# Norm rows made in the projection, output weights split around the last store, and a modulation folded into the router's weights

## The reference

```python
h_lat = modulate(rms_norm(x, norm_g[l, 0]), mod_lat[0], mod_lat[1])
m_ctx, m_lat = hybrid_mixer(h_ctx, h_lat, w_in[l], ...)
x = x + mod_lat[2] * rms_norm(m_lat, norm_g[l, 1])

h_lat = modulate(rms_norm(x, norm_g[l, 2]), mod_lat[3], mod_lat[4])
y_lat = ec_moe(h_lat, router_w[l], exp_w_gate[l], exp_w_up[l], exp_w_down[l])
x = x + mod_lat[5] * rms_norm(y_lat, norm_g[l, 3])
```

## Time and profile before

| | us |
|---|---|
| runs | 1444.17, 1443.9, 1441.17; median 1443.9 |
| profiled execution | 1444.64 (span of the core's instructions 1442.9) |
| PE busy | 1291.1 (89%) |
| DVE busy | 780.1 (54%) |
| ACT busy | 468.2 (32%) |
| POOL busy | 230.2 (16%) |
| DMA, mean over the span | 188 GB/s |
| mean granted clock of TensorE | 0.955 of full |

### The profile page before, as it was taken

How to read it: one execution, slowest core, us unless ns; L and a number is a source line. 1 busy time by engine, 2 the same in 40 slices (tenths; PEclk the granted TensorE clock), 3 DMA queues, 4 the chain that set the end, 5 groups by cost and what they waited for, 6 DMA issues and landing times.

```text
span 1442.9 us, 13834 instructions
## 1 busy us (share of the span) xinstructions
PE 1291.1 (89%) x5008; PEld 748.6 (52%) x5008; DVE 780.1 (54%) x1102; ACT 468.2 (32%) x1101; POOL 230.2 (16%) x206
## 2 busy tenths in 40 slices
PE   6999999899999999899999878997079999999993
PEld 2444554445545555689889744454034444444441
DVE  4169888797874877487767555553910010010015
ACT  4335543542211112667766523333011101101122
POOL 0004111121000000174455200000010110101111
PEclk9999999999999999999999989997579999999996
DMA  9515354345223443366556644432749999999967
GB/s 367 124 29 177 114 153 138 95 141 153 88 87 103 84 88 79 81 185 189 180 171 186 240 161 174 157 134 100 266 165 350 327 341 342 324 341 338 330 228 173
DMA packets 207529, 270.64 MB, mean 188 GB/s; under 512 B 75053, under 2 KB 124198, under 8 KB 207462
## 3 DMA queue, kind: packets, MB, share of 16 engines
q1 hardware_dynamic: 187118, 210.97, 45.1%
q0 software_dynamic: 14272, 52.43, 12.1%
q10 hardware_dynamic: 6072, 6.35, 1.2%
HBM read 217.75 MB, written 51.97 MB: 187 GB/s over the span
## 4 chain that ended last, share of the span: by engine, by line
PE 59%; DMA 13%; DVE 12%; ACT 11%; issue 4%; SPq 2%; POOL 0%; POOLq 0%; ACTq 0%; DVEq 0%
PE ps L1820 25%; PE ps L1078 13%; PE ps L1097 6%; DMA arena<-g_dram 5%; DMA arena<-zt_dram 2%; DVE arena L2167 2%; PE ps L387 2%; ACT arena L524 2%; PE ps L1041 2%; DMA y_dram<-arena 2%; DMA arena<-ada_w 2%; ACT arena L533 2%; PE ps L1695 1%; PE ps L1773 1%; ACT arena L513 1%
## 5 line engine op out<-in xcount | busy, mean ns | idle before, releaser
L1820 PE MATMUL ps<-arena 128*128 128x512 f32 (+1 forms) x1072 | 424.8, 553 | 0.0
L1820 PEld LDWEIGHTS ps<-arena 128*128 128x128 f32 x1072 | 202.4, 191 | 202.4 <-issue 197.4
L1078 PE MATMUL ps<-arena 128*128 128x512 f32 x512 | 227.3, 597 | 1.4 <-ACT arena L1200 1.4
L2167 DVE SCALAR_TENSOR_TENSOR arena<-arena,taps 128x1024 f32<-128x1024 f32 x160 | 215.9, 1349 | 5.5
L1078 PEld LDWEIGHTS ps<-arena 128*128 128x128 f32 x512 | 96.7, 192 | 117.1 <-issue 115.1
L387 PE MATMUL ps<-arena 128*128 128x128 f32 x1080 | 135.5, 281 | 17.1 <-DVE arena L604 13.3
L387 PEld LDWEIGHTS ps<-arena 128*128 128x128 f32 x1080 | 130.4, 195 | 23.7 <-DVE arena L604 16.4
L1363 DVE TENSOR_TENSOR arena<-arena,ps 128x512 f32<-128x512 f32 x16 | 11.0, 688 | 224.4 <-PE ps L1078 224.4
L1041 PE MATMUL ps<-arena 128*128 128x512 f32 x256 | 115.6, 606 | 4.6 <-ACT arena L1149 4.6
L1097 PE MATMUL ps<-arena 128*128 128x512 f32 x256 | 113.3, 595 | 0.0
L1041 PEld LDWEIGHTS ps<-arena 128*128 128x128 f32 x256 | 48.3, 193 | 62.5 <-issue 55.8
(11 more groups left out here) (298 smaller groups left out, 1634.8 us busy)
## 6 DMA issues: line engine op xcount, KB each, us to landing
arena<-exp_w_gate SPq DMA_DIRECT2D x16, 2048.0 KB, 11.1
arena<-exp_w_up SPq DMA_DIRECT2D x16, 2048.0 KB, 9.1
arena<-exp_w_down SPq DMA_DIRECT2D x16, 2048.0 KB, 11.1
arena<-ada_w POOLq DMA_DIRECT2D x16, 1024.0 KB, 6.4
arena<-w_in SPq DMA_DIRECT2D x28, 512.0 KB, 5.2
arena<-ada_w SPq DMA_DIRECT2D x4, 2048.0 KB, 18.0
arena<-x SPq DMA_DIRECT2D x16, 512.0 KB, 6.6
arena<-g_dram SPq DMA_DIRECT2D x16, 512.0 KB, 4.7
```

The source lines that it names most:

```text
L1078: last = mm(ps[gu_bank[s] + j][:], xsT[s][:, k, :], ew[s][j][:, k, :], start=(k == 0), stop=(k == KD - 1))
L1820: last = mm(ps[3 * (m % 2) + gi][:, 0:w], wring[(m + 1) % NW][:, k, :], hT[:, k, o:o + w], start=(k == 0), stop=(k == KD - 1))
L2167: ins = v.scalar_tensor_tensor(accg, cin_l[ci % 2][:, j // 3:j // 3 + GR, j % 3:j % 3 + GW], tp[:, j:j + 1], accg, ALU.mult, ALU.add)
```

## The change

- The columns `rcol` of the norms are made on DVE between the scan's preparation and the first `v` convolution. There, the router's weights are also multiplied by the second modulation's gain (`rwg`). A new job `rows` in block `M_V0 + 2` = 21 transposes the columns into 32 rows, which ACT copies and stores to `rows_dram`, and multiplies the shift by the router's weights into `shifted` (eight products of 16 columns).
- In the tail, SP loads `rowv` and `row5` from there, spread over the partitions. The 32 transposes and eight copies go.
- `scan_over` goes from PE's and ACT's tails, and on DVE it moves behind `front_r(2)`. Tile 0's `front` moves into DVE's last scan step, ahead of `y_diag`.
- `w_out` lies in two separate halves. The first is loaded after the last use of the first direction's buffers, ahead of the last two scan stores, the second after the last but one store has landed, ahead of the last store.
- `front_r(t+1)` stands behind `front(t+1)` and so ahead of `back_sum(t-1)`.
- `h2` is only scaled by the root, no longer by the gain, and without the shift: the router uses `rwg` and adds `shifted`; ACT's copy of an expert's turned tokens applies gain and shift per column block, in four operations instead of one.
- ACT's squares go to another scrap buffer (`sqf` in place of `sqj`), in the places that the cut diff leaves out too.

```diff
@@ -59,6 +59,7 @@
     tok_dram = dram("tok_dram", (DN_H + 1, NT * P, P))
+    rows_dram = dram("rows_dram", (4 * (D // P), P))
@@ -263,11 +264,19 @@
             jobs[m] += [("late", i, 0)]
+        jobs[M_V0 + 2] += [("rows", 0, 0)]
...
+        rcol = arena[:, 49152:49152 + 4 * KD].rearrange("p (r k) -> p r k", r=4)
+        rowst = arena[0:4 * KD, 49152 + 4 * KD:49152 + 4 * KD + P]
+        rwg = arena[:, 49152 + 160:49152 + 160 + KD * E_N].rearrange("p (k n) -> p k n", k=KD)
+        shifted = arena[:, 49152 + 160 + KD * E_N:49152 + 160 + (KD + 1) * E_N]
@@ -677,6 +686,9 @@
                 if lat(own):
+                    if s == 2 * NS - 1:
+                        dve_front(dve, link, 0)
@@ -861,10 +873,14 @@
         h2T = [take(D).rearrange("p (k n) -> p k n", k=KD) for _ in range(2)]
-        rowv = take(3 * D).rearrange("p (r n) -> p r n", r=3)
+        rowv = take(D)
+        sqf = take(D)
+        sq, rs, sm = ([take(8) for _ in range(2)] for _ in range(3))
...
         at[0] = W0
-        wo = take(KD * D).rearrange("p (k n) -> p k n", k=KD)
+        wo = [take(KD * 512).rearrange("p (k n) -> p k n", k=KD) for _ in range(2)]
...
@@ -943,14 +957,25 @@
                 sp_.dma_start(xr[s], x_t[o]).then_inc(sem(f"xr_in{s}"), 16)
+            def load_wo(h):
+                sp_.dma_start(wo[h], wo_k[:, :, h * 512:(h + 1) * 512]).then_inc(sem(f"wo_in{h}"), 16)
+            def load_row(dst, r):
+                sp_.dma_start(dst, rows_dram[r * KD:(r + 1) * KD].rearrange("k p -> (k p)").unsqueeze(0).to_broadcast([P, D]))\
+                    .then_inc(sem("rowv"), 16)
...
             load(1)
-            for step in steps[-2:]:
-                scan_store(sp_, step)
+            sp_.wait_ge(sem("s_op"), turn(0, NL))
+            load_wo(0)
+            scan_store(sp_, steps[-2])
+            sp_.wait_ge(sem("st_o0"), 16 * NL)
+            load_wo(1)
+            scan_store(sp_, steps[-1])
+            sp_.wait_ge(sem("rows_out"), 16)
+            load_row(rowv, 0)
             scan_over(sp_)
-            for h in range(2):
-                sp_.dma_start(wo[:, :, h * 512:(h + 1) * 512], wo_k[:, :, h * 512:(h + 1) * 512])\
-                    .then_inc(sem(f"wo_in{h}"), 16)
+            load_row(row5, 3)
@@ -989,19 +1014,6 @@
             mm, tr = nc.tensor.matmul, nc.tensor.transpose
-            scan_over(pe)
-            for r in range(4):
-                if r >= 2:
-                    pe.wait_ge(sem("rowv"), r - 1)
-                elif r == 0:
-                    pe.wait_ge(sem("rcol"), 1)
-                for k in range(KD):
-                    last = tr(ps[2 * (r % 2) + k // 4][:, (k % 4) * P:(k % 4 + 1) * P], rcol[:, r, k:k + 1].to_broadcast([P, P]),
-                              ident[:])
-                last.then_inc(sem("rowps"), 1)
-            pe.wait_ge(sem("rowv"), 4)
...
@@ -1038,7 +1050,7 @@
                     for k in range(KD):
-                        last = mm(ps[2 + 2 * s + h][:], mixT[s][:, k, :], wo[:, k, h * 512:(h + 1) * 512],
+                        last = mm(ps[2 + 2 * s + h][:], mixT[s][:, k, :], wo[h][:, k, :],
@@ -1122,7 +1134,6 @@
             a = nc.scalar.activation
-            scan_over(act)
@@ -1131,9 +1142,9 @@
                 for h in range(DN_H):
-                    a(sqj[:, h * P:(h + 1) * P], fb[s][:, h * P:(h + 1) * P], ACT.Square, accum_out=sq[s][:, h:h + 1])
+                    a(sqf[:, h * P:(h + 1) * P], fb[s][:, h * P:(h + 1) * P], ACT.Square, accum_out=sq[s][:, h:h + 1])
                 for g in range(SSM_G):
-                    last = a(sqj[:, QK + g * 256:QK + (g + 1) * 256], fb[s][:, QK + g * 256:QK + (g + 1) * 256],
+                    last = a(sqf[:, QK + g * 256:QK + (g + 1) * 256], fb[s][:, QK + g * 256:QK + (g + 1) * 256],
...
@@ -1197,7 +1208,9 @@
                     act.wait_ge(sem("gu"), 2 * e - 2)
-                a(xsT[e % 2][:, 4 * h:4 * h + 4, :], heads(ps[0][:]), ACT.Copy).then_inc(sem("xsT"), 1)
+                for k in range(4 * h, 4 * h + 4):
+                    last = a(xsT[e % 2][:, k, :], ps[0][:, cols(k % 4)], ACT.Identity, scale=rcol[:, 1, k:k + 1], bias=rcol[:, 2, k:k + 1])
+                last.then_inc(sem("xsT"), 1)
@@ -1231,27 +1244,17 @@
+        def dve_front(dve, link, t):
+            v = nc.vector
+            s = t % 2
+            dve.wait_ge(sem(f"m_in{s}"), 64 * (t // 2 + 1))
+            link(v.tensor_tensor(fb[s], fb[s], bb[s], ALU.add))
+            link(v.tensor_tensor(heads(bb[s][:, QK:D], SSM_H), heads(xtok[:, ORD[t], :], SSM_H), bc(sbc[:, 48:56], SSM_P), ALU.mult))
+            link(v.tensor_tensor(fb[s][:, QK:D], fb[s][:, QK:D], bb[s][:, QK:D], ALU.add))
+            v.tensor_tensor(fb[s][:, QK:D], fb[s][:, QK:D], zb_[s], ALU.mult).then_inc(sem("merged"), 1)
...
             v = nc.vector
-            scan_over(dve)
-            m = mods[:, :, 0]
-            g = vcols[:, V_NG:V_CB].rearrange("p (r k) -> p r k", k=KD)
-            link(v.tensor_tensor(m[:, 2 * KD:6 * KD], m[:, 2 * KD:6 * KD], vcols[:, V_AB + 2 * KD:V_NG], ALU.add))
-            v.tensor_tensor(rcol[:, 0, :], m[:, 2 * KD:3 * KD], g[:, 1, :], ALU.mult)
-            v.scalar_tensor_tensor(rcol[:, 1, :], m[:, 4 * KD:5 * KD], 1.0, g[:, 2, :], ALU.add, ALU.mult)
-            v.tensor_copy(rcol[:, 2, :], m[:, 3 * KD:4 * KD])
-            v.tensor_tensor(rcol[:, 3, :], m[:, 5 * KD:6 * KD], g[:, 3, :], ALU.mult).then_inc(sem("rcol"), 1)
-            def front(t):
-                s = t % 2
-                dve.wait_ge(sem(f"m_in{s}"), 64 * (t // 2 + 1))
-                link(v.tensor_tensor(fb[s], fb[s], bb[s], ALU.add))
-                link(v.tensor_tensor(heads(bb[s][:, QK:D], SSM_H),
-                                     xtok[:, ORD[t], :].rearrange("p (h n) -> p h n", h=SSM_H),
-                                     bc(sbc[:, 48:56], SSM_P), ALU.mult))
-                link(v.tensor_tensor(fb[s][:, QK:D], fb[s][:, QK:D], bb[s][:, QK:D], ALU.add))
-                v.tensor_tensor(fb[s][:, QK:D], fb[s][:, QK:D], zb_[s], ALU.mult).then_inc(sem("merged"), 1)
@@ -1279,7 +1282,7 @@
                     hs_ = slice(h * 512, (h + 1) * 512)
-                    ins = v.scalar_tensor_tensor(x2[:, ORD[t], hs_], ps[2 + 2 * s + h][:], sm[s][:, 2:3], rowv[:, 0, hs_],
+                    ins = v.scalar_tensor_tensor(x2[:, ORD[t], hs_], ps[2 + 2 * s + h][:], sm[s][:, 2:3], rowv[:, hs_],
@@ -1292,21 +1295,20 @@
                     dve.wait_ge(sem("h2ps"), t - 1)
-                link(v.scalar_tensor_tensor(h2[s], x2[:, ORD[t], :], sm[s][:, 3:4], rowv[:, 1, :], ALU.mult, ALU.mult))
-                v.tensor_tensor(h2[s], h2[s], rowv[:, 2, :], ALU.add).then_inc(sem("h2"), 1)
-            front(0)
-            for r in range(4):
-                dve.wait_ge(sem("rowps"), r + 1)
-                dst = rowv[:, r, :] if r < 3 else row5
-                v.tensor_copy(dst[:, 0:512], ps[2 * (r % 2)][:])
-                v.tensor_copy(dst[:, 512:D], ps[2 * (r % 2) + 1][:]).then_inc(sem("rowv"), 1)
+                v.tensor_scalar(h2[s], x2[:, ORD[t], :], sm[s][:, 3:4], None, ALU.mult).then_inc(sem("h2"), 1)
+            front_r(0)
...
                 if t < NL:
-                    front_r(t)
...
                 if t + 1 < NL:
-                    front(t + 1)
+                    dve_front(dve, link, t + 1)
+                    front_r(t + 1)
+                if t == 1:
+                    scan_over(dve)
+                    dve.wait_ge(sem("rowv"), 16)
@@ -1314,7 +1316,7 @@
                     o = ORD[t - 2]
-                    v.tensor_copy(aff[:, o % 4 * 2 + o // 4, :], ps[1][:, 0:E_N]).then_inc(sem("lcopy"), 1)
+                    v.tensor_tensor(aff[:, o % 4 * 2 + o // 4, :], ps[1][:, 0:E_N], shifted, ALU.add).then_inc(sem("lcopy"), 1)
@@ -1800,6 +1802,12 @@
                                           start=True, stop=True)
+                    elif kind == "rows":
+                        pe.wait_ge(sem("rcol"), 1)
+                        tr(bank[0:4 * KD, 0:P], rcol.rearrange("p r k -> p (r k)"), ident[:])
+                        for k in range(KD):
+                            last = mm(bank[:, P:P + E_N], rcol[:, 2, k:k + 1].to_broadcast([P, P]), rw[:, k, :],
+                                      start=(k == 0), stop=(k == KD - 1))
@@ -1961,11 +1969,17 @@
                                  bank[:].rearrange("p (q g n) -> p q g n", q=2, g=SSM_G), ACT.Copy)
+                    elif kind == "rows":
+                        a(shifted, bank[:, P:P + E_N], ACT.Copy)
+                        last = a(rowst, bank[0:4 * KD, 0:P], ACT.Copy)
...
-                    if kind == "qk":
+                    if kind == "rows":
+                        act.wait_ge(sem("aux_used"), aux + 1)
+                        act.dma_start(rows_dram, rowst).then_inc(sem("rows_out"), 16)
+                    elif kind == "qk":
@@ -2241,6 +2255,15 @@
             dve.wait_ge(sem("g_dve"), 7)
+            mc = mods[:, :, 0]
```

(16 more changed lines are left out.)

## The result

| | before | after |
|---|---|---|
| median of runs, us | 1444.4 (20 runs) | 1453.2 (20 runs) |
| ratio | | 1.0054, 95% interval 1.0042 to 1.0066 |
| profiled execution, span, us | 1442.9 | 1448.0 |
| PE / DVE / ACT busy, us | 1291.1 / 780.1 / 468.2 | 1292.3 / 761.0 / 497.9 |

The changed kernel is slower by 0.5%, and the forecast was 1437.0. The profiled execution of after (1449.8) is one of its quicker ones, so its trace shows 5.1 us of a difference that is 8.8 us by the medians.

What follows compares the result with a forecast made beforehand. Bound: the tail's per-tile loop through load transfers, not PE. Handover 9.0, order -2.0, product 4.2, last h2 1.8, rows -2.0, copies -1.95, stores -2.0: 7.05 us gained, so 1437.0 us, range 1432.5 to 1441.5.

Steps and rivals of the forecast that it cites:

- rows in the projection: In the projection, PE's added transpose and eight 16-column products lie wholly on the path: 2.0 us lost, at most 3.
- handover, to A(2): Between scan and tail: tile 0 done 9.9 us sooner, 0.9 lost waiting for tile 2's loads: 9.0 us gained.
- A(2): In the tail's tile loop: the time at which DVE starts to merge tile 2; likewise for other tile numbers.
- new order on DVE, five loops: In the tail loop, scaling the next tile ahead of the sum adds 0.4 us per loop: 2.0 us lost.
- stores against loads, five loops: In the tail loop, earlier stores of h2 and x2 meet the next loads: 0.4 us per loop, 2.0 us lost.
- product of tile 7 behind A(7): In the tail, each product starts sooner after its tile's merge because h2 is ready earlier: 4.2 us gained, once.
- h2 of the last tile: At the stage's end, tile 7's h2 lies bare on the chain and gets shorter: 1.8 us gained.
- copies in the experts: In the experts, four ACT operations replace one, 0.65 us more per group, three groups bare: 1.95 us lost.
- rival 5: Tail loop: 1 MB of stores ahead of the loads' last bytes makes the kernel slower, 1448 at the bound; chance 0.04.
- c: Tail loop: extra time per loop from stores meeting loads; taken as 0.4 us, between 0 and 2.6.
- my bound of 2.6: Tail loop: most extra us per loop, if all 1 MB of stores goes ahead of the loads' last bytes, twice 1.3.
- Rival 3: Tail loop: stores and loads share alike, 1.85 us more overlap at half rate; 1439.4, up to 1441; chance 0.15.

Runs made afterwards that it cites:

- the second one: The changed kernel run again with no edit, beside the kernel before: 1454.97 us, ratio 1.0051.
- the run with the earlier loads: Changed kernel with the next tile's four loads issued ahead of the wait for the residual's buffer: 1434.24 us, ratio 0.991 to the kernel before.
- the kernel before with the hold: Kernel before, with GpSimd sending tile t's stores only after tile t+3's loads have landed: 1446.38 us, ratio 1.0009.

## Why the prediction was wrong

Step by step, in the profiled executions (plus is gained, us):

| step | forecast | measured |
|---|---|---|
| rows in the projection | -2.0 | -1.9 |
| handover, to A(2) | +9.0 | +8.0 |
| new order on DVE, five loops | -2.0 | -1.5 |
| stores against loads, five loops | -2.0 | -8.0 |
| product of tile 7 behind A(7) | +4.2 | +2.9 |
| h2 of the last tile | +1.8 | +1.8 |
| copies in the experts (-2.7), first gate product (-1.0) | -1.95 | -3.7 |
| head, projection and scan otherwise | 0 | -3.0 |
| sum | +7.05 | -5.4 (spans: -5.1) |

**The step that failed** is the paragraph "An unknown: stores against loads". That earlier stores lengthen the wait for the next loads was named, and so was rival 5, which decides from c = 1.8 and had 0.04. The term c was mis-sized: I took 0.4; in the profiled execution it was 1.6 (9.5 us less the order's 1.5, over five), in the second one 2.7 ((109.9 - 95.0) / 5 less 0.3), past my bound of 2.6; with the stores at once on ScalarE's queue it was 3.6. Two reasonings led there. I read the landings of 6.08 to 7.07, with stores 2.75 us behind, as a measure of how much overlap costs, though the stores hardly overlap the loads there: in the transfer view of before, 909 to 917.04, that is until 1.4 us behind the store's issue, 1.75 of the loads' 2.10 MB have gone, and no packet of the stores. In after it is 1.09 MB at the same distance from the store's issue, where the slow stretch begins. The view by queue of before could have told the first of these ahead of the run. And my bound counted the stores' bytes at the loads' full rate, which holds only if the rate stays up; it does with loads, and does not with stores. Rival 3 had stores and loads share at half rate each. By the packets they take turns only at the end: the Trainium skill (DMA: Bandwidth & Descriptors, Queues, rings and completion order) states turns between queues, and the run with loads in the stores' place agrees for the last packets (8.3 to 9.0 us against 6.2). It does not explain the slow stretch of after, in which one queue's packets run alone for 3.5 us; every run with stores at the early place has such a fall.

**The second miss** is the product of tile 7, +2.9 instead of +4.2. Its row in after:

```profile
976.63 1.07 PE L1041 MATMUL ps<-ident,arena 128*128 128x128 f32 x8 [1.54 <-DVE arena L1319]
```

L1319 is the router's copy. PE's transposes wait for it because it frees their bank, and on DVE it stands behind h2. I had followed the scaling and h2, not this wait; the run with that copy first shows the 1.4 us.

**The third** is the copies, with their rows:

```profile
1058.37 1.50 ACT L1212 ACTIVATE arena<-ps,arena 128x128 f32<-128x128 f32 x4 [44.00 <-PE ps L1079]
1061.09 1.51 ACT L1212 ACTIVATE arena<-ps,arena 128x128 f32<-128x128 f32 x4 [1.21 <-PE ps L1079]
```

1.51 us a group, where I took 1.25: 0.91 more than the one copy's 0.60, three times. I had gone by the four copies with a gain alone, for which the chain of before has this row:

```profile
842.74 1.15 ACT arena L1149 x4
```

A shift as a second operand per partition adds 0.36 to a group. The Trainium skill (ScalarE: Activation LUTs, What ACT_TABLE_LOAD costs) says that each such operand adds about 93 ns to an operation, an estimate of 0.37 us for four; these rows agree, and the term would have been 0.9 instead of 0.65. Another 1.0 us is the first gate product: 10.16 us at a granted clock of 0.70, against 9.19 at 0.77 at the same place before. No run ties it to the change: the product took 8.91 to 10.12 us in twelve other executions with the change and the four copies, and 8.76 to 9.82 in three others without the change.

**What was right:** the handover (product 10.0 us earlier against 10.6, PE's wait 0.52 against 0.6, DVE's 0.96 against 0.9), the rows' job, the end of the stage, and that only three groups of copies lie bare.

**What stays open:** some 3 us in the scan's first steps in the kernels with the change (0.8 in the profiled execution of after), where VectorE waits for loads of `g_dram` (3.66 us before one of them in the run with the earlier loads, 2.48 before). The tensor's address is excluded; nothing else was tried. The 2.1 us that after is late by 447 us needn't be the change's: the kernel before with the hold, whose edit acts only in the tail, had 1.7 of them. Why issued stores slow the loads' packets before any of their own is recorded is open too, and so is why 0.4 us of distance decides so much in the run with loads in their place.

## What to carry to other kernels

Making an engine faster moves what it sets off. Before shortening the step that releases a store, look at which load is in flight at the new time, and who waits for it; if the chain of waits goes through that load, hold the store until it has landed, or fetch a loop earlier. A landing time read at one distance between two streams says nothing about another distance: 1.8 us decided here between 6.5 and 8.5 to 10 us.

## What the runs showed of the hardware

- Stores issued 0.7 to 1.0 us behind the last of the loads lower the rate: 168 to 300 GB/s for 3 to 3.5 us, against some 360 to 440 in before and with a second stream of loads. It was so on GpSimd's, ScalarE's and SyncE's queues. In after the packets of this stretch (914.5 to 918 us) are all the loads' own, 0.85 MB; the stores' run from 918 on.
- When the second stream's packets run, the last packets of the first lie between them: with loads on both queues, the last 87 (0.04 MB) of the waited-for ones took from 920 us until about 923.
- 1 MB of stores in two transfers lands 3.8 us behind the second issue when held behind the loads; issued beside the loads, in after, it takes 8.8 us.
- A second stream's effect changed steeply with its distance: loads issued 0.97 us behind the waited-for one made it land after 8.3 to 9.0 us, 1.35 us behind after 6.2 and 6.5.
